# Down weights of a mixture of experts asked for by ScalarE's queue, up weights by SyncE's

## What is computed

```python
def expert_block(args):
    xb, e = args
    return (jax.nn.silu(xb @ w1[e]) * (xb @ w3[e])) @ w2[e]
```

## Time and profile before

| | us |
|---|---|
| median of 3 runs | 1753.58 (1753.31 to 1756.1) |
| the profiled execution | 1755.25 |
| its span, first to last instruction | 1753.5 |
| busy: TensorE, VectorE, ScalarE | 1689.2, 1441.5, 941.7 |
| up weights: pieces asked for, median to landing | 128, 21.6 |
| down weights: pieces asked for, median to landing | 64, 22.1 |
| results stored, median to landing | 31, 6.9 |

### The profile page before, as it was taken

How to read it: one execution, slowest core, us unless ns; L and a number is a source line. 1 busy time by engine, 2 the same in 40 slices (tenths; PEclk the granted TensorE clock), 3 DMA queues, 4 the chain that set the end, 5 groups by cost and what they waited for, 6 DMA issues and landing times. The chain is left out here.

```text
span 1753.5 us, 24119 instructions
## 1 busy us (share of the span) xinstructions
PE 1689.2 (96%) x8776; PEld 1276.4 (73%) x8776; DVE 1441.5 (82%) x2045; ACT 941.7 (54%) x1218; POOL 159.7 (9%) x137
## 2 busy tenths in 40 slices
PE   7999999999999999999999999999999999999990
PEld 7768888877777777777778788877777777777760
DVE  6687958988789988678828986689898989898997
ACT  6533122133344555555566532277777777878762
POOL 1100000000000000000000000032212122222103
PEclk9999999999999999999999999999999999999995
DMA  5202132122354422412315941399999999999967
GB/s 210 72 1 85 54 111 88 61 84 73 108 189 131 139 69 67 144 55 67 127 37 211 331 170 66 141 375 392 404 389 402 395 404 396 402 396 399 404 273 287
DMA packets 77040, 359.82 MB, mean 205 GB/s; under 512 B 9020, under 2 KB 11612, under 8 KB 50588
## 3 DMA queue, kind: packets, MB, share of 16 engines
q1 hardware_dynamic: 67372, 325.14, 49.5%
q0 software_dynamic: 5888, 20.97, 3.6%
q10 hardware_dynamic: 3696, 12.59, 1.8%
HBM read 301.63 MB, written 55.99 MB: 204 GB/s over the span
## 5 line engine op out<-in xcount | busy, mean ns | idle before, releaser
L2798 DVE TENSOR_TENSOR wa_lo<-wa,w_hi 128x2048 fp32r<-128x2048 f32 x124 | 280.6, 2285 | 12.7 <-ACT w_hi L2682 11.7
L2682 ACT ACTIVATE w_hi<-wa 128x2048 fp32r<-128x2048 f32 x124 | 237.4, 1915 | 61.3 <-PE psum L2610 30.6
L1608 PE MATMUL psum<-h_hi,w_hi 128*128 128x512 f32 x510 | 210.7, 413 | 1.4 <-ACT gate_out L1270 0.9
L1608 PE MATMUL psum<-h_hi,w_lo 128*128 128x512 f32 x510 | 204.3, 401 | 0.0
L1608 PE MATMUL psum<-h_lo,w_hi 128*128 128x512 f32 x510 | 202.3, 397 | 0.0
L176 DVE MAX8 top<-sel 128x8 f32<-128x384 f32 (+5 forms) x192 | 171.3, 892 | 4.6
L174 DVE MATCH_REPLACE8 sel<-top,sel 128x384 f32<-128x384 f32 (+5 forms) x192 | 168.1, 876 | 0.0
L2806 DVE TENSOR_TENSOR wb_lo<-wd,w_hi 128x2048 fp32r<-128x2048 f32 x62 | 139.3, 2288 | 31.2 <-ACT w_hi L2692 31.2
L2578 PE MATMUL psum<-w_hi,xT_hi 128*96 128x512 f32 x508 | 162.8, 401 | 0.0
L2578 PE MATMUL psum<-wa_lo,xT_hi 128*96 128x512 f32 x512 | 160.5, 394 | 0.0
L2578 PE MATMUL psum<-w_hi,xT_lo 128*96 128x512 f32 x508 | 158.9, 394 | 0.0
(11 more groups left out here) (404 smaller groups left out, 3327.3 us busy)
## 6 DMA issues: line engine op xcount, KB each, us to landing
wa<-expert_up SPq DMA_DIRECT2D x128, 1024.0 KB, 21.6
wd<-expert_down SPq DMA_DIRECT2D x64, 1024.0 KB, 22.1
w<-w_gate SPq DMA_DIRECT2D x32, 512.0 KB, 4.1
gate_pre<-gate_out SPq DMA_DIRECT2D x64, 256.0 KB, 3.5
gate<-gate_pre SPq DMA_DIRECT2D x32, 512.0 KB, 6.2
ys<-yo ACTq DMA_DIRECT2D x31, 384.0 KB, 6.9
w<-w_T SPq DMA_DIRECT2D x18, 512.0 KB, 3.8
ys<-zeros SPq DMA_DIRECT2D x7, 1152.0 KB, 5.9
```

What stands on the lines that cost most here:

```text
L1608: ins = nc.tensor.matmul(psum[:, 7, :], w[:, k, :], x[:, k, half * 512:(half + 1) * 512], start=(n == 0), stop=(n == BURST - 1))
L2682: nc.scalar.activation(hi_a(i, j, q).rearrange("p c m n -> p (c m n)"), wa[j][q][:, :, :, :].rearrange("p c m n -> p (c m n)"), ACT.Copy). ...
L2798: nc.vector.tensor_tensor(wa_lo[j][q][:, :, :, :].rearrange("p c m n -> p (c m n)"), wa[j][q][:, :, :, :].rearrange("p c m n -> p (c m n)" ...
```

## The change

ScalarE's queue asks for both down pieces of expert e+2 in `y_out` of expert e, after its wait for both halves of the down matmuls of e and ahead of the copy `yo`. SyncE's `refill` keeps the up weights alone. The down weights of experts 0 and 1 are asked for elsewhere, as before.

```diff
     def sync(sp):
-        def refill(i, j, up, down):
-
-            if up:
-                for q in range(4):
-                    sp.wait_ge(a_used, i * 8 + (4 * j - 8 + q + 1))
-                    s.load_a(sp, i * 2 + j, j, q)
-            if down:
-                for q in range(2):
-                    sp.wait_ge(b_used, i * 4 + (2 * j - 6 + q + 1))
-                    s.load_b(sp, i * 2 + (j - 1), 1 - j, q)
-
-        refill(1, 1, True, True)
+        def refill(i, j):
+
+            for q in range(4):
+                sp.wait_ge(a_used, i * 8 + (4 * j - 8 + q + 1))
+                s.load_a(sp, i * 2 + j, j, q)
+
+        refill(1, 1)
         with sp.Fori(2, NE // 2) as i:
             for j in range(2):
-                refill(i, j, True, True)
-        refill(NE // 2, 0, False, True)
+                refill(i, j)
 
@@ scalar, y_out
         def y_out(i, j, first):
 
             act.wait_ge(b_used, i * 4 + (2 * j + 2))
+            if not isinstance(i, int) or i * 2 + j + 2 < NE:
+                for q in range(2):
+                    s.load_b(act, i * 2 + (j + 2), j, q)
             if not first:
                 act.wait_ge(y_stored[j], i * 16)
             nc.scalar.activation(yo[j][:, :], y_banks().rearrange("p a b -> p (a b)"),
```

## The result

The changed kernel takes 1762.11 us (median of 7 runs, 1759.94 to 1766.11), the one before 1753.31 (7 runs beside them, 1751.87 to 1756.1). The ratio is 1.0053, 95% interval 1.0042 to 1.0063: slower by 8.8 us. The forecast was 1757.4 with a range of 1752.6 to 1763.5. The direction was right and the time lies in the stated range, but the loss is more than twice the 3.8 worked out and lies outside the forecast's own +1.2 to +6.2. It is close to the 9.4 of rival B, for whose sake the range reached that far.

What follows compares the result with a forecast made beforehand. TensorE was taken to bound the loop, with the DMA engines full too. Queue growth of 3.7 us plus 0.1 for the gather, and 0 for issuing, gave +3.8 us on 1753.58: 1757.4, range 1752.6 to 1763.5.

Steps and rivals of the forecast that it cites:

- rival B: Gather's stretch: ys moves later beside the gather, the queue grows 0.2 us more a period; +9.4 us, 1763.0, chance 0.17.
- TensorE bounds, weights come just in time: Expert loop: TensorE's period is 17.62 us without idle time; DMA engines need about 17.8, the difference paid from slack.
- budget of q=3 23.03 + 2.3 us: Fourth up piece: 23.03 us from request to need, then 2.3 us tolerated lateness before TensorE stalls at hid.
- ScalarE's issuing costs nothing: ScalarE ahead of yo: the two requests fit under the q=3 copy; 0 us, bounds 0 and 1.3.
- Down weights alternate with up weights and land early: DMA queues: down weights alternate with up-weight packets, landing nearly 8 us ahead of need.
- q=3 is overtaken by 5.0 us: DMA queues: all down weights of the batch go ahead of the fourth up piece, which lands 5.0 us later.
- When the requests go out: ScalarE's program: down requests leave at about 1419.7 and 1420.1, 2.6 and 0.4 us later than before.
- What the queue grows: Loop from 1326 on: TensorE loses the queue's growth, 0.22 us a period, up to landing time 24.0; 3.7 us.
- B's sign: Gather's stretch: a fall of its GB/s would show that ys moving there costs rate.
- Rival A: TensorE in the loop: q=3's lateness never reaches it, so not slower; 1753.6 within 1 us, chance 0.29.

Runs made afterwards that it cites:

- e8: The kernel before, with one 64 KB store an expert added on SyncE's queue behind both down pieces; ratio 1.002.
- e3: The changed kernel with the gathers of experts 2 to 31 replaced by plain loads of 64 bytes a row; ratio 0.9996.
- e11: The changed kernel with the two down requests moved ahead of ScalarE's copy of the fourth up piece; ratio 1.0012.
- e10: The changed kernel with the gather waiting for the first down piece of the batch under way, for experts 2 and 3 alone; ratio 1.0036.
- the four slow kernels: The changed kernel and three variants of it: gather asked for later, fourth up piece on ScalarE too, down requests behind yo's store; 1.0053, 1.0053, 1.0069, 1.0066.
- e2: The changed kernel with only the second down piece asked for by ScalarE, the first staying with SyncE; ratio 0.9994.

## Why the prediction was right or wrong, point by point

- **TensorE bounds, weights come just in time; budget of q=3 23.03 + 2.3 us**: right. The stall came by the chain that was named, at hid; it began between landing times of 25.4 and 25.8 in e8, and between 25.5 and 25.9 in the changed kernel (the pieces asked for at 1184 and at 1219). So it came with the piece of 1219 and not, as forecast, with that of 1326.
- **ScalarE's issuing costs nothing**: right (0.86 us under the copy of q=3; e3). Laid open, as in e11, it costs 0.7 us, all at the last expert.
- **Down weights alternate with up weights and land early; q=3 is overtaken by 5.0 us**: right in kind, and near in size: 6.0 at 1202, and 5.2 to 5.5 in e11's first experts. Down weights land in 11.1 us as the page's median (8 to 14 forecast), mostly 9.1 for the first piece of a pair and 16 for the second; ys in 16.5 (15 or more).
- **When the requests go out**: here a step failed. The prediction had them at TensorE's pace, "at about 1419.7 and 1420.1", and said of the wait that "nothing new is queued behind it", because it looked at one semaphore, `b_used`. The copy of q=3 ahead of them waits also for the landing of its own piece, and in the changed kernel that wait is 3.4 us. The requests were put behind exactly the wait that the change makes longer. e11 against the changed kernel is the price of that: 1.0012 against 1.0053.
- **"What the queue grows"**: the term of the sum that was wrong. It took the growth of 0.22 us a period from the kernel before and held it fixed, so order alone was to give +3.7. In e11 and e10 the growth is negative, and in the changed kernel it is about 0.48 (18.1 less 17.62). What the order alone costs is small and not well known: the runs of e11 give 2.1 us (0.2 to 2.2 in a thousand of the time, 0.4 to 3.9 us), but its profiled loop has no period that the order made longer, and 0.7 us of it is the issues' at the last expert. The rest of the 8.8, three quarters by these medians, is rate. Order is what starts it: it takes q=3 from 19.0 to 25.5 us and so makes ScalarE's copy late.
- **Rival B** got the size and the kind (rate lost where the gather moves) and had the wrong culprit: it blamed ys moving beside the gather. Between 1300 and 1600 of the changed kernel ys never does. In e11 it does, and the engines then lose less, as the last section shows. The culprit is the second stream of 8 KB packets, which meets the gather in the four slow kernels alone. B's sign, a fall of the rate in the gather's stretch, is not there either (327 GB/s before, 336 in the changed kernel as the mean of its stretches between 1300 and 1600): it is the stretch that grew, from 3.8 to 5.9 us an expert. So the measured time lies in the stated range by luck in part: the forecast's own bounds, 1754.8 to 1759.8, miss it, and what took the range to 1763.5 was a price of B for something that did not happen.
- **Rival A** lives on in e2: with one piece moved, ScalarE waits 61 us and TensorE not at all.
- **Rate by arrangement**: with two weight queues the engines yield what they yield with one, 424 GB/s and 419. With the gather as third, where the requests stand changed the mean of 1300 to 1600 from 391 to 406 GB/s (399 before). The Trainium skill says (DMA: Bandwidth & Descriptors, Rules for kernel authors) that spreading transfers over issuing engines does not help bandwidth, since they interleave on the same 16 engines. The first pair of numbers agrees, and the changed kernel's mean is no gain either. The rule doesn't speak of which transfers meet, and between 391 and 406, both with the same issuing engines, that is all that differs.

The 10.1 us of the profiled loop are more than the 8.8 of the spans. The stages ahead of the loop differ by some us from execution to execution (its first transposes lie at 1159.55 and 1160.65 in the two), and nothing was made of that part.

**Why GpSimd's copy and its gather instruction are short in some kernels.** The traces answer this. Here are VectorE's `wb_lo` and GpSimd around the gather, in the kernel before first and then in the changed one:

```profile
1407.87 4.49 DVE L2806 TENSOR_TENSOR wb_lo<-wd,w_hi 128x2048 fp32r<-128x2048 f32 x2 [1.12 <-ACT w_hi L2692]
1408.74 1.47 POOL L2547 COPY idx<-tok_of 96x1 int32 x1 [13.25 <-PE psum L2434]
1411.01 2.17 POOL L2538 DMA_INDIRECT xg<-h_rows,idx  x1 [0.80 <-POOL idx L2547]
```

```profile
1411.27 0.51 POOL L2541 COPY idx<-tok_of 96x1 int32 x1 [15.71 <-PE psum L2434]
1412.58 0.94 POOL L2532 DMA_INDIRECT xg<-h_rows,idx  x1 [0.80 <-POOL idx L2541]
1413.38 4.49 DVE L2803 TENSOR_TENSOR wb_lo<-wd,w_hi 128x2048 fp32r<-128x2048 f32 x2 [1.17 <-ACT w_hi L2686]
```

In the kernel before, both start while VectorE is at a subtraction of weight pieces (`wb_lo`, twice 2.3 us). In the changed kernel the gather's instruction starts ahead of it. In all twelve kernels, between 1200 and 1690, the 118 idx copies that start outside such a subtraction take 0.18 us each and the 100 gather instructions 0.94 us each; all longer ones start during one (up to 4.45 and 3.06 us). So a late q=3 piece works twice. It makes ScalarE's down requests late, by 2.7 us at 1209.83. And it makes `wb_lo` late, out of GpSimd's way, so that the gather's first packet moves 2.4 us sooner after the transposes of the hidden rows (1.3 us in the request, 1.1 in the instruction). From the first down request to the gather's first packet it is 14.2 us at TensorE's pace and 9.1 us here; from that expert on some 95 down packets move within each gather, where the one before had 3. e11 takes away the first part, and its gather instruction is at 2.34 us again; no run holds back one of the two parts and leaves the other, so their shares are not shown.

## What to carry to other kernels

A request for a transfer inherits every wait that stands ahead of it on its engine, landings too: here 3.4 us of a late piece. When a load is moved to another engine's queue, look for the transfer which that engine waits for just before, and ask whether the move makes it later: if so, it feeds back. Put requests ahead of waits that may grow, at the pace of the engine that frees the buffer. And where DMA engines are full, a growth per period read from a trace is not a constant of the kernel: it depends on which transfers meet, so it has to be worked out anew for the new order, or left as a range.

## What the runs showed of the hardware

What the gather meets decides what it costs. From e11, 1253 to 1256 (gather, ys and up weights) and 1447 to 1450 (gather and up weights, hardly any ys):

```profile
DMA packets 236, 1.22 MB, mean 408 GB/s; under 512 B 10, under 2 KB 10, under 8 KB 163
...
DMA packets 203, 1.00 MB, mean 332 GB/s; under 512 B 37, under 2 KB 37, under 8 KB 126
```

Beside 8 KB weight packets alone, from one queue or from two, the engines yield 318 to 332 GB/s, and each 8 KB packet takes 400 to 440 ns instead of 313. With the 4 KB packets of the store of ys between them they yield 408 in that stretch, and the 8 KB packets take 310 to 330 (383 GB/s as the mean of all such stretches of e11 between 1300 and 1600, 404 in e10). Two thirds of e11's gather time falls on the store, and it moves more bytes than any other (406 GB/s, where TensorE's pace asks for 402): so it could work off its queue. Why a store between helps was not tried.
